# Gate and up products of an FFN: one product of 512 columns and one of 256 in place of three of 256

## Chip, cores and metric

The kernel runs on one core of one Trainium2 chip. The metric is the device time of one execution in microseconds. Every number in this part is of the kernel before the change.

## The reference

Two model blocks are computed one behind the other on 256 tokens of width 1024, each block with two layers. All is float32. Only the feed-forward networks (FFNs) are touched by the change:

```python
D_MODEL, SEQ, DEPTH, D_FF = 1024, 256, 2, 2816

def swiglu(x, w_gate, w_up, w_down):                 # first block
    return (jax.nn.silu(x @ w_gate) * (x @ w_up)) @ w_down

def _swiglu(h, w_in, w_out):                         # second block
    g, u = jnp.split(h @ w_in, 2, axis=-1)
    return (jax.nn.silu(g) * u) @ w_out

# first block, each layer
x = layer_norm(ALPHA * x + 0.5 * swiglu(x, ffn1...), ...)
...  # in-projection, pooling, convolution, attention, out-projection, layer_norm
x = layer_norm(ALPHA * x + 0.5 * swiglu(x, ffn2...), ...)
# second block, each layer
x = x + 0.5 * _rmsnorm(_swiglu(_rmsnorm(x, ng[0]), w_ffn_in[l, 0], w_ffn_out[l, 0]), ng[1])
...  # three mixers, branch gates, attention to a memory
x = x + 0.5 * _rmsnorm(_swiglu(_rmsnorm(x, ng[6]), w_ffn_in[l, 1], w_ffn_out[l, 1]), ng[7])
```

So there are eight FFNs: two in each of two layers of each of two blocks.

## The kernel before

**High and low halves.** TensorE takes float32r operands, which hold fewer bits than float32. To keep the precision, each operand is split in two: the high half is the value rounded to float32r, and the low half is the rest. A product is then the sum of three matmuls into the same PSUM bank: high by high, high by low, low by high. The helper `three` (L389, L390, L391) issues them for a weight of 128x128 and an activation of 128 (contraction) by 256 (tokens); its `left` is the weight's pair, its `right` the activation's pair. `three_rows` (L405 to L407) does the same with 512 moving columns. In it the activation is the stationary operand and the weight streams.

**Weight pieces.** Weights come in pieces of 128x1024 values (512 KB). A piece goes through four steps in the order of its number e. SyncE issues its DMA into one of 6 raw buffers (`sp_load`, L354). ScalarE copies it with rounding into `w_hi`, one of 3 slots (`act_split`, L702); for this it waits until piece e-3 has been used. VectorE subtracts it into `w_lo` (`low_part`, L913). TensorE waits for `split_low` and multiplies.

**The activations** of an FFN lie transposed in `in_hi` and `in_lo`, 8 tiles (KD) of 128 features by 256 tokens.

**An FFN** (`pe_ffn`, `act_ffn`, `dve_ffn`) runs over 22 tiles of 128 hidden features. Each tile has three pieces: gate, up and down. In steady state TensorE runs gate(j), up(j), down(j-1), gate(j+1), and so on. Gate and up take 8 values of k times `three`, 24 matmuls a piece; both results share a PSUM bank, `FFN_BANK[j % 2]`, as its two halves. Down takes 12 matmuls of 512 columns, from `hid_hi` and `hid_lo`, and accumulates in banks 0 to 3 over all tiles. Tile 0 is done by `begin`, which goes through gate and up together, two k at a time, as the activations arrive.

**Beside TensorE.** The order on ScalarE and VectorE is written out by `ffn_steps`, which calls `after(e, ...)` once for each piece e. In the first block ScalarE takes the silu of the gate out of PSUM (L752), and `hidden` on VectorE multiplies it by the up result in PSUM (L1014), rounds it to `hid_hi` (L1016) and subtracts for `hid_lo` (L1018). In the second block the RMS norm's factor is folded in behind the products (`fold`): VectorE first multiplies gate and up by `rstd` out of PSUM into `gate_up` (L1002, L1004), and silu and `hidden` work on that. `rstd` is made by a small product, `spread`, after tile 0.

**Seeded starts.** In three of the four FFNs of the first block VectorE writes the scaled residual into banks 0 to 3 (`dve_ln_seed`, L1099 and L1104). The second half of that (`second_seed`) is issued in `after(2)`, and the first down step waits for it.

## Time and profile before

| | us |
|---|---|
| median of three runs | 2785.0 (2780.41, 2785.0, 2787.51) |
| the profiled execution | 2780.14 |
| its span, first to last instruction | 2778.3 |
| mean granted TensorE clock | 0.993 of full speed |

The rows below come from the profiled execution alone. PE is TensorE's matmuls, PEld its weight loads, DVE is VectorE, ACT ScalarE, POOL GpSimd, and SPq the queue that issues DMAs. Matmuls are pipelined: the record of one lasts until its last result is written, so records overlap, and the sum of their lengths is more than the time. In a timeline the first number is the start, the second the length. Idle time and its releaser stand in brackets.

### The profile page before, as it was taken

To read this page: it belongs to the slowest core of one execution; us is meant where nothing else is said; L and a number is where in the kernel's file an instruction comes from. 1 tells how busy PE (TensorE), PEld (TensorE's weight loads), DVE (VectorE), ACT (ScalarE), POOL (GpSimd) and SP (SyncE) were. 2 spreads that over 40 slices of the span, in tenths; PEclk is the share of its full clock that TensorE was granted. 3 is DMA by queue.
4 is the path that set the end of the run, shared out by engine and by line. 5 is a ranking of instruction groups with operands and counts; after the bars stand their busy time and mean duration, and the time that the engine had idled before them with its cause. 6 is when DMAs were issued, how large, how long until landed. Compare 5 with 4: busy or idle time off the path is not lost.

```text
span 2778.3 us, 51978 instructions
## 1 busy us (share of the span) xinstructions
PE 2707.1 (97%) x21524; PEld 2499.6 (90%) x21524; DVE 1708.8 (62%) x2552; ACT 1306.4 (47%) x1855; POOL 217.4 (8%) x95
## 2 busy tenths in 40 slices
PE   8999999999999999999999999999999999999998
PEld 7999699899978989999899898999999889989998
DVE  5557755755757566666742756667665763375666
ACT  4445543434454444456633456445446642455543
POOL 0000000000000000005225000000002422300000
PEclk9999999999999999999999999999999999999999
DMA  8765366577545656664323554666664421464664
GB/s 238 210 194 160 98 189 186 172 221 195 165 122 164 184 158 183 186 193 122 102 75 107 167 182 122 196 181 178 186 203 133 128 85 55 160 189 133 177 184 128
DMA packets 622972, 445.41 MB, mean 160 GB/s; under 512 B 28048, under 2 KB 589488, under 8 KB 622320
## 3 DMA queue, kind: packets, MB, share of 16 engines
q1 hardware_dynamic: 622832, 443.43, 54.6%
q8 instruction: 102, 1.67, 0.2%
q14 instruction: 38, 0.31, 0.0%
HBM read 442.32 MB, written 1.05 MB: 160 GB/s over the span
## 4 chain that ended last, share of the span: by engine, by line
PE 88%; DVE 9%; ACT 2%; issue 1%; DMA 0%; SPq 0%; DVEq 0%; ACTq 0%
PE ps L389 19%; PE ps L391 18%; PE ps L390 18%; PE ps L405 7%; PE ps L406 7%; PE ps L407 7%; DVE w_lo L913 2%; PE ps L687 1%; PE ps L663 1%; PE ps L1661 1%; PE ps L1651 1%; ACT sq L1153 1%; DVE moments L1066 1%; PE ps L1623 1%; DVE sq L970 1%
## 5 line engine op out<-in xcount | busy, mean ns | idle before, releaser
L389 PE MATMUL ps<-in_hi,w_hi 128*128 128x256 f32 x4352 | 1248.7, 287 | 33.5 <-DVE in_lo L990 10.7
L913 DVE TENSOR_TENSOR w_lo<-raw,w_hi 128x1024 fp32r<-128x1024 f32 x705 | 862.1, 1225 | 647.2 <-ACT w_hi L702 646.2
L391 PE MATMUL ps<-in_hi,w_lo 128*128 128x256 f32 x4352 | 1234.5, 284 | 0.0
L390 PE MATMUL ps<-in_lo,w_hi 128*128 128x256 f32 x4352 | 1234.4, 284 | 0.0
L702 ACT ACTIVATE w_hi<-raw 128x1024 fp32r<-128x1024 f32 x800 | 845.0, 1057 | 794.7 <-PE ps L391 545.0
L389 PEld LDWEIGHTS ps<-in_hi,w_hi 128*128 128x128 f32 x4352 | 837.0, 192 | 56.2 <-issue 11.7
L390 PEld LDWEIGHTS ps<-in_lo,w_hi 128*128 128x128 f32 x4352 | 837.2, 192 | 7.2 <-issue 0.5
L391 PEld LDWEIGHTS ps<-in_hi,w_lo 128*128 128x128 f32 x4352 | 836.9, 192 | 0.0
L913 POOL TENSOR_TENSOR w_lo<-raw,w_hi 128x1024 fp32r<-128x1024 f32 x90 | 216.9, 2412 | 2176.3 <-ACT w_hi L702 2176.3
L405 PE MATMUL ps<-w_hi,hid_hi 128*128 128x512 f32 x704 | 276.5, 393 | 1.1 <-DVE ps L1104 1.1
L406 PE MATMUL ps<-w_lo,hid_hi 128*128 128x512 f32 x704 | 276.1, 392 | 0.0
L407 PE MATMUL ps<-w_hi,hid_lo 128*128 128x512 f32 x704 | 274.1, 389 | 0.0
L407 PEld LDWEIGHTS ps<-w_hi,hid_lo 128*128 128x128 f32 x704 | 132.3, 188 | 28.7
L405 PEld LDWEIGHTS ps<-w_hi,hid_hi 128*128 128x128 f32 x704 | 132.9, 189 | 25.4 <-DVE ps L1104 2.4
L406 PEld LDWEIGHTS ps<-w_lo,hid_hi 128*128 128x128 f32 x704 | 132.9, 189 | 21.2
L752 ACT ACTIVATE work<-work 128x256 f32<-128x256 f32 x88 | 37.0, 420 | 198.1 <-DVE work L1002 198.1
L752 ACT ACTIVATE work<-ps 128x256 f32<-128x256 f32 x88 | 33.7, 383 | 154.3 <-PE ps L391 154.3
L961 DVE TENSOR_TENSOR in_lo<-arena,in_hi 128x512 fp32r<-128x512 f32 x44 | 31.7, 744 | 93.0 <-ACT in_hi L708 92.8
L1018 DVE TENSOR_TENSOR hid_lo<-work,hid_hi 128x256 fp32r<-128x256 f32 x176 | 74.9, 426 | 6.0
L405 PE MATMUL ps<-w_hi,in_hi 128*128 128x512 f32 x192 | 75.6, 394 | 1.1 <-ACT std L830 1.1
L407 PE MATMUL ps<-w_hi,in_lo 128*128 128x512 f32 x192 | 74.8, 390 | 0.0
L406 PE MATMUL ps<-w_lo,in_hi 128*128 128x512 f32 x192 | 74.8, 389 | 0.0
(341 smaller groups left out, 2693.8 us busy)
## 6 DMA issues: line engine op xcount, KB each, us to landing
raw<-in_w_ffn_in SPq DMA_DIRECT2D x176, 512.0 KB, 3.9
raw<-in_w_mix SPq DMA_DIRECT2D x112, 512.0 KB, 3.8
raw<-in_ffn_w_gate SPq DMA_DIRECT2D x88, 512.0 KB, 4.0
raw<-in_ffn_w_up SPq DMA_DIRECT2D x88, 512.0 KB, 3.8
raw<-in_ffn_w_down SPq DMA_DIRECT2D x88, 512.0 KB, 3.6
raw<-in_w_ffn_out SPq DMA_DIRECT2D x88, 512.0 KB, 4.2
raw<-in_w_in SPq DMA_DIRECT2D x40, 512.0 KB, 3.8
raw<-in_w_out SPq DMA_DIRECT2D x32, 512.0 KB, 3.8
```

The lines of the kernel that those rows point to most:

```text
L389: nc.tensor.matmul(o, lh, rh, start=first, stop=False, **kw)
L390: nc.tensor.matmul(o, lh, rl, start=False, stop=False, **kw)
L391: return nc.tensor.matmul(o, ll, rh, start=False, stop=last, **kw)
L405: nc.tensor.matmul(o, left_hi[:, tok], right_hi, start=first, stop=False, **kw)
L406: nc.tensor.matmul(o, left_hi[:, tok], right_lo, start=False, stop=False, **kw)
L407: return nc.tensor.matmul(o, left_lo[:, tok], right_hi, start=False, stop=last, **kw)
L663: mm = nc.tensor.matmul(ps[:, 4 + i % 2, t * S:(t + 1) * S], q, k, start=(m == 0), stop=(m == len(pieces) - 1))
L702: nc.scalar.activation(w_hi[:, e % SPLIT, :], raw[:, e % RAW, :], ACT.Copy).then_inc(sem("split_high"), 1)
L752: nc.scalar.activation(silu[:, up % 2, :], src, ACT.Silu).then_inc(sem("silu_ready"), 1)
L913: eng.tensor_tensor(w_lo[:, e % SPLIT, :], raw[:, e % RAW, :], w_hi[:, e % SPLIT, :].bitcast(F32), ALU.subtract)\
L961: nc.vector.tensor_tensor(in_lo[:, lo:hi, :], src[:, 2 * c:2 * c + 2, :], in_hi[:, lo:hi, :].bitcast(F32), ALU.subtract).then_inc(sem("in_ ...
L1018: nc.vector.tensor_tensor(hid_lo[:, j, :], hid[:, j, :], hid_hi[:, j, :].bitcast(F32), ALU.subtract)\
```

## The change

From tile 1 on, gate and up get a bank each (`gate_up_bank`, four banks in rotation). For each k the high half of the weight multiplies the high and the low activations in one matmul of 512 columns: `in_hi` and `in_lo` become the two halves of one tensor, `in_both`, so that they are next to each other for each k. Its first 256 results are high by high, the other 256 high by low. The low half of the weight by the high activations is then accumulated onto the first 256. So a piece has 16 matmuls in place of 24, and its result lies in two halves that have to be added.

For the sum, ScalarE copies the second half out of PSUM into `part` (in `taken`, semaphore `part_taken`), and VectorE adds it to the first half into `gate_up` (in `whole_of`, semaphore `summed`). In the second block VectorE then multiplies the sum in place by `rstd` (`scaled`). Silu and `hidden` read `gate_up` instead of PSUM. The gate's half is taken and added in `after(3j-1)`, the up's in `after(3j)`. Tile 0 keeps its three products and takes bank 4 (`FIRST_BANK`); the bank of `spread` moves from 6 to 5. The list of semaphore names is changed to match and left out here.

```diff
@@ -169,7 +169,8 @@
         ps = ctx.enter_context(nc.psum_tensor("ps", [P, 8, 512], F32))
         raw = sb("raw", [P, RAW, PIECE])
         w_hi, w_lo = (sb(n, [P, SPLIT, PIECE], F32R) for n in ("w_hi", "w_lo"))
-        in_hi, in_lo = (sb(n, [P, KD, S], F32R) for n in ("in_hi", "in_lo"))
+        in_both = sb("in_both", [P, KD, 2, S], F32R)
+        in_hi, in_lo = (in_both[:, :, i, :] for i in range(2))
         hid_hi, hid_lo = (sb(n, [P, 2, S], F32R) for n in ("hid_hi", "hid_lo"))
         const = sb("const", [P, CONST_N])
         ones = sb("ones", [P, S])
...
@@ -187,6 +188,7 @@
         att_p = work[:, 4 * S:12 * S].rearrange("p (b c t) -> p b c t", b=4, c=2)
         att_pT = work[:, 12 * S:16 * S].rearrange("p (b c t) -> p b c t", b=2, c=2)
         diag = work[:, 8 * S:9 * S].rearrange("p (t c) -> p t c", t=HALF)
+        part = work[:, 9 * S:13 * S].rearrange("p (j a t) -> p j a t", j=2, a=2)
         first_gains = sb("first_gains", [P, LAYERS, KD])
         spare = sb("spare", [P, 2])
         moments = sb("moments", [P, HALF, 2, 6])
...
@@ -427,7 +429,7 @@
 
         WARM_BANK = 7
         TURN_BANK = 4
-        SPREAD_BANK = 6
+        SPREAD_BANK = 5
 
         def pe_warm(pe, n):
...
@@ -469,7 +471,19 @@
         given = (in_hi, in_lo)
 
 
-        FFN_BANK = (4, 5)
+        FIRST_BANK = 4
+
+        def gate_up_bank(j, i):
+
+            return ps[:, 4 + 2 * (j % 2) + i, :]
+
+        def summed(f, j, i):
+
+            return 2 * (f * (TILES - 1) + j - 1) + i + 1
+
+        def scaled(fold, j, i):
+
+            return 2 * (fold * TILES + j) + i + 1
 
         def pe_ffn(pe, n, e0, chunk, seeds=None, fold=None):
...
@@ -486,23 +500,24 @@
                             pe.wait_ge(sem("split_low"), e0 + i + 1)
                         w = piece(e0 + i)
                         for k in (2 * c, 2 * c + 1):
-                            mm = three(ps[:, FFN_BANK[i // 2], i % 2 * S:(i % 2 + 1) * S], at2(w, ALL, k, ALL),
-                                       at2(given, ALL, k, ALL), k == 0 and i % 2 == 0, k == KD - 1, skip_group_check=True)
+                            mm = three(ps[:, FIRST_BANK, i * S:(i + 1) * S], at2(w, ALL, k, ALL),
+                                       at2(given, ALL, k, ALL), k == 0 and i == 0, k == KD - 1, skip_group_check=True)
                         if c == KD // 2 - 1:
                             mm.then_inc(sem("piece_used"), 1)
 
             def gate_up(j, it=0):
                 for i in range(2):
-                    if 2 * j + i < TOGETHER:
-                        continue
-                    e = e0 + max(3 * j - 1, 0) + i
+                    e = e0 + 3 * j - 1 + i
 
                     pe.wait_ge(sem("split_low"), e + 1 + it * RAW)
-                    w = piece(e)
+                    hi, lo = piece(e)
+                    bank = gate_up_bank(j, i)
                     for k in range(KD):
 
-                        mm = three(ps[:, FFN_BANK[j % 2], i * S:(i + 1) * S], at2(w, ALL, k, ALL), at2(given, ALL, k, ALL),
-                                   k == 0, k == KD - 1)
+                        nc.tensor.matmul(bank.rearrange("p (a t) -> p a t", a=2), hi[:, k, :], in_both[:, k, :, :], start=(k == 0),
+                                         stop=False, skip_group_check=True)
+                        mm = nc.tensor.matmul(bank[:, 0:S], lo[:, k, :], in_hi[:, k, :], start=False, stop=(k == KD - 1),
+                                              skip_group_check=True)
                     mm.then_inc(sem("piece_used"), 1)
 
             def down(j, it=0, last=False):
...
@@ -738,17 +753,29 @@
         def act_ffn(act, n, e0, fold=None):
 
 
-            def after(e, up=None, whole=None, it=0):
+            def taken(e, i, j, it):
+
+                act.wait_ge(sem("piece_used"), e0 + e + 1 + it * RAW)
+                nc.scalar.activation(part[:, j % 2, i, :], gate_up_bank(j, i)[:, S:2 * S], ACT.Copy)\
+                    .then_inc(sem("part_taken"), 1)
+
+            def after(e, up=None, whole=None, it=0, gate=None):
+                if gate:
+                    taken(e, 0, gate, it)
+                if up:
+                    taken(e, 1, up, it)
                 if up == 0 and fold is not None:
                     act.wait_ge(sem("spread_ready"), fold + 1)
                     nc.scalar.activation(rstd[:, :], ps[:, SPREAD_BANK, 0:S], ACT.Copy).then_inc(sem("rstd_ready"), 1)
                 if up is not None:
+                    src = gate_up[:, up % 2, 0, :]
                     if fold is not None:
-                        act.wait_ge(sem("gate_scaled"), fold * TILES + up + 1 + it * 2)
-                        src = gate_up[:, up % 2, 0, :]
+                        act.wait_ge(sem("scaled"), scaled(fold, up, 0) + it * 4)
+                    elif up:
+                        act.wait_ge(sem("summed"), summed(ffn0 + n, up, 0) + it * 4)
                     else:
-                        act.wait_ge(sem("piece_used"), e0 + e + 1 + it * RAW)
-                        src = ps[:, FFN_BANK[up % 2], 0:S]
+                        act.wait_ge(sem("piece_used"), e0 + e + 1)
+                        src = ps[:, FIRST_BANK, 0:S]
                     nc.scalar.activation(silu[:, up % 2, :], src, ACT.Silu).then_inc(sem("silu_ready"), 1)
                 if e < FFN_PIECES - 1 and e0 + e + SPLIT < E_LAST:
                     act_split(act, e0 + e + SPLIT, it)
...
@@ -765,7 +792,7 @@
                     after(0)
                     after(1, 0, 0)
                     return
-                after(3 * j - 1, None, None, it)
+                after(3 * j - 1, None, None, it, gate=j)
                 after(3 * j, j, None, it)
                 after(3 * j + 1, None, j, it)
...
@@ -994,22 +1021,33 @@
         def dve_ffn(dve, n, e0, second_seed=lambda: None, fold=None):
 
 
-            def scaled(e, up, it):
-                j = up % 2
-                if up == 0:
-                    dve.wait_ge(sem("rstd_ready"), fold + 1)
-                dve.wait_ge(sem("piece_used"), e0 + e + 1 + it * RAW)
-                nc.vector.tensor_tensor(gate_up[:, j, 0, :], ps[:, FFN_BANK[j], 0:S], rstd[:, :], ALU.mult)\
-                    .then_inc(sem("gate_scaled"), 1)
-                nc.vector.tensor_tensor(gate_up[:, j, 1, :], ps[:, FFN_BANK[j], S:2 * S], rstd[:, :], ALU.mult)\
-                    .then_inc(sem("up_scaled"), 1)
+            def first_scaled(e):
+
+                dve.wait_ge(sem("rstd_ready"), fold + 1)
+                dve.wait_ge(sem("piece_used"), e0 + e + 1)
+                for i in range(2):
+                    nc.vector.tensor_tensor(gate_up[:, 0, i, :], ps[:, FIRST_BANK, i * S:(i + 1) * S], rstd[:, :], ALU.mult)\
+                        .then_inc(sem("scaled"), 1)
+
+            def whole_of(e, i, j, it):
+
+                o = gate_up[:, j % 2, i, :]
+                dve.wait_ge(sem("part_taken"), summed(ffn0 + n, j, i) + it * 4)
+                nc.vector.tensor_tensor(o, gate_up_bank(j, i)[:, 0:S], part[:, j % 2, i, :], ALU.add).then_inc(sem("summed"), 1)
+                if fold is not None:
+                    dve.wait_ge(sem("summed"), summed(ffn0 + n, j, i) + it * 4)
+                    nc.vector.tensor_tensor(o, o, rstd[:, :], ALU.mult).then_inc(sem("scaled"), 1)
 
             def hidden(whole, it):
                 j, count = whole % 2, (ffn0 + n) * TILES + whole + 1 + it * 2
+                up = gate_up[:, j, 1, :]
                 if fold is not None:
-                    dve.wait_ge(sem("up_scaled"), fold * TILES + whole + 1 + it * 2)
+                    dve.wait_ge(sem("scaled"), scaled(fold, whole, 1) + it * 4)
+                elif whole:
+                    dve.wait_ge(sem("summed"), summed(ffn0 + n, whole, 1) + it * 4)
+                else:
+                    up = ps[:, FIRST_BANK, S:2 * S]
                 dve.wait_ge(sem("silu_ready"), count)
-                up = ps[:, FFN_BANK[j], S:2 * S] if fold is None else gate_up[:, j, 1, :]
 
                 nc.vector.tensor_tensor(hid[:, j, :], silu[:, j, :], up, ALU.mult).then_inc(sem("hidden_whole"), 1)
                 dve.wait_ge(sem("hidden_whole"), count)
...
@@ -1018,9 +1056,13 @@
                 nc.vector.tensor_tensor(hid_lo[:, j, :], hid[:, j, :], hid_hi[:, j, :].bitcast(F32), ALU.subtract)\
                     .then_inc(sem("hidden_ready"), 1)
 
-            def after(e, up=None, whole=None, it=0):
-                if up is not None and fold is not None:
-                    scaled(e, up, it)
+            def after(e, up=None, whole=None, it=0, gate=None):
+                if up == 0 and fold is not None:
+                    first_scaled(e)
+                elif up:
+                    whole_of(e, 1, up, it)
+                elif gate:
+                    whole_of(e, 0, gate, it)
                 if up == 0 and fold is None:
 
                     hidden(whole, it)
```

## Rows read from the trace of the kernel before

**Rows 1.** The page, parts 1 and 2: busy time, and the granted clock in 40 slices.
```profile
PE 2707.1 (97%) x21524; PEld 2499.6 (90%) x21524; DVE 1708.8 (62%) x2552; ACT 1306.4 (47%) x1855; POOL 217.4 (8%) x95
...
PEclk9999999999999999999999999999999999999999
```

**Rows 2.** The page, part 4: the chain that ended last, by engine and line.
```profile
PE 88%; DVE 9%; ACT 2%; issue 1%; DMA 0%; SPq 0%; DVEq 0%; ACTq 0%
PE ps L389 19%; PE ps L391 18%; PE ps L390 18%; PE ps L405 7%; PE ps L406 7%; PE ps L407 7%; DVE w_lo L913 2%; PE ps L687 1%; PE ps L663 1%; PE ps L1661 1%; PE ps L1651 1%; ACT sq L1153 1%; DVE moments L1066 1%; PE ps L1623 1%; DVE sq L970 1%
```

**Rows 3.** The page, part 5: groups, with count, busy us, mean ns, idle before.
```profile
L389 PE MATMUL ps<-in_hi,w_hi 128*128 128x256 f32 x4352 | 1248.7, 287 | 33.5 <-DVE in_lo L990 10.7
...
L752 ACT ACTIVATE work<-work 128x256 f32<-128x256 f32 x88 | 37.0, 420 | 198.1 <-DVE work L1002 198.1
L752 ACT ACTIVATE work<-ps 128x256 f32<-128x256 f32 x88 | 33.7, 383 | 154.3 <-PE ps L391 154.3
```

**Rows 4.** Timeline of TensorE, one tile, first block: start us, us, engine, line, operation.
```profile
151.35 0.40 PE L405 MATMUL ps<-w_hi,hid_hi 128*128 128x512 f32 x1
151.59 0.40 PE L406 MATMUL ps<-w_lo,hid_hi 128*128 128x512 f32 x1
...
152.74 0.39 PE L405 MATMUL ps<-w_hi,hid_hi 128*128 128x512 f32 x1
...
154.10 0.28 PE L389 MATMUL ps<-in_hi,w_hi 128*128 128x256 f32 x1
154.21 0.28 PE L390 MATMUL ps<-in_lo,w_hi 128*128 128x256 f32 x1
...
159.85 0.40 PE L405 MATMUL ps<-w_hi,hid_hi 128*128 128x512 f32 x1
```

**Rows 5.** Busy time by stretch: one tile of each block, columns in the first row.
```profile
core 0: us, PE busy (x) PEld busy (x) DVE busy (x) ACT busy (x) POOL busy (x), PEclk, DMA share, GB/s
151.35:159.85 8.50, 8.50 (x62) 8.01 (x61) 4.73 (x6) 3.45 (x4) 0.00 (x0) 1.00 0.74 199
1803.00:1811.50 8.50, 8.50 (x62) 8.01 (x62) 5.49 (x8) 3.49 (x4) 0.00 (x0) 1.00 0.63 184
```

**Rows 6.** Timeline of ScalarE and VectorE in the tile of rows 4.
```profile
151.55 0.38 ACT L752 ACTIVATE work<-ps 128x256 f32<-128x256 f32 x1 [1.82 <-PE ps L391]
...
152.92 1.23 DVE L913 TENSOR_TENSOR w_lo<-raw,w_hi 128x1024 fp32r<-128x1024 f32 x1 [1.93 <-ACT w_hi L702]
...
156.53 0.41 DVE L1014 TENSOR_TENSOR work<-work,ps 128x256 f32<-128x256 f32 x1
...
157.31 0.43 DVE L1018 TENSOR_TENSOR hid_lo<-work,hid_hi 128x256 fp32r<-128x256 f32 x1
```

**Rows 7.** Timeline, last tile of an FFN of the second block, all engines.
```profile
2764.77 0.42 DVE L1002 TENSOR_TENSOR work<-ps,rstd 128x256 f32<-128x256 f32 x1 [0.50 <-PE ps L391]
...
2765.23 0.42 ACT L752 ACTIVATE work<-work 128x256 f32<-128x256 f32 x1 [2.22 <-DVE work L1002]
...
2765.75 0.42 DVE L1014 TENSOR_TENSOR work<-work 128x256 f32<-128x256 f32 x1 [0.22 <-ACT work L752]
...
2766.53 0.43 DVE L1018 TENSOR_TENSOR hid_lo<-work,hid_hi 128x256 fp32r<-128x256 f32 x1
...
2767.32 0.39 PE L405 MATMUL ps<-w_hi,hid_hi 128*128 128x512 f32 x1
```

**Rows 8.** Timeline at a seeded FFN start: TensorE, then VectorE.
```profile
345.65 0.50 PE L405 MATMUL ps<-w_hi,hid_hi 128*128 128x512 f32 x1 [0.37 <-DVE ps L1104]
...
342.87 1.40 DVE L1099 SCALAR_TENSOR_TENSOR zT<-ps,mean_var,arena 128x512 f32<-128x512 f32 x2
...
346.23 3.50 DVE L913 TENSOR_TENSOR w_lo<-raw,w_hi 128x1024 fp32r<-128x1024 f32 x3
```

**Rows 9.** The same, with the columns of rows 5, of one slow stretch.
```profile
280.00:287.00 7.00, 6.87 (x20) 3.93 (x19) 5.57 (x14) 4.56 (x13) 0.00 (x0) 0.55 0.43 146
```

More of the change, by code:

```diff
@@ L162, in build @@
                  "split_high", "split_low", "piece_used", "in_high", "in_ready", "turn_in", "turned", "rows_out", "silu_ready",
-                 "hidden_whole", "hidden_high", "hidden_ready", "tok_stat", "tok_std", "x_ready", "post_scaled", "diag_ready", "spread_ready", "rstd_ready", "gate_scaled", "up_scaled", "vector_step", "ln_here",
+                 "hidden_whole", "hidden_high", "hidden_ready", "tok_stat", "tok_std", "x_ready", "post_scaled", "diag_ready", "spread_ready", "rstd_ready", "scaled", "part_taken", "summed", "vector_step", "ln_here",
                  "gains_here", "ln_cols_here", "opened", "seeded", "ln_scale", "ln_turned", "ln_act", "ln_vec", "post_here0", "post_here1", "post_here2", "post_here3") + \
```

## Prediction

> **What bounds the kernel now.** I read the busy times and the granted clock first. TensorE is busy for 97% of the span, VectorE for 62%, ScalarE for 47%, and the clock row is at 9 tenths or more in all 40 slices [rows 1]. Then the chain that ended last: 88% of it is TensorE, 9% VectorE, 2% ScalarE, and three lines of one helper, L389 to L391, hold 19, 18 and 18% of the span [rows 2]. Those are the 128x256 products that the change rewrites. So wherever TensorE runs without a gap, what the change gives is what it takes out of TensorE's own stream; work added on VectorE and ScalarE counts only where TensorE then waits for it.
>
> The recorded mean of a matmul can't be used for its price: it is 287 ns at L389 [rows 3], while the products start every 120 ns, so the records overlap. I take differences of start times. Between the first gate product of a tile at 154.10 and the first down product at 159.85 lie 48 products of 256 columns: 5.75/48 = 0.1198 us each. The 12 products of 512 columns of the down step go from 151.35 to 154.10: 0.2292 each; the last six of them, from 152.74, take 1.36/6 = 0.2267, and the first six 1.39/6 = 0.2317 [rows 4]. The period of a tile is 8.50 us, in which TensorE is always busy, in the first block and in the second alike [rows 5].
>
> So one product of 512 columns with the same weights costs 0.2267 where two of 256 cost 2 x 0.1198 = 0.2396. The whole case for the change is this difference of 12.9 ns; twice the columns are still streamed.
>
> **What the change takes out.** Per weight piece and k, three products of 256 columns become one of 512 and one of 256. The silu appears 88 + 88 = 176 times, once a tile, so eight FFNs of 22 tiles [rows 3]. Tile 0 of each keeps the old form, which leaves 8 x 21 x 2 pieces x 8 k = 2688 such triples. Old price: 3 x 0.1198 = 0.3594. New price from the settled rows: 0.2267 + 0.1198 = 0.3465. Saving: 12.9 ns x 2688 = 34.7 us. No row of before shows 512 and 256 columns in turn, so this is the unknown cost. From below: the first 256-column product behind a run of 512 starts its successor after only 0.11 (154.10 to 154.21), which would make a pair 0.337 and the saving 61 us. From above: the first 512 behind a run of 256 takes 0.24 (151.35 to 151.59), a pair of 0.36 and no saving; the mean of the first six gives 0.3515, 7.9 ns and 21 us [rows 4]. In the new order each 512 follows a 256 and each 256 follows a 512, so the two edge effects (0.24 up, 0.11 down) meet in every pair: 0.35 together. That is why I take the settled 0.3465 and neither end.
>
> **What it adds on ScalarE.** One copy of 128x256 out of PSUM for each of the 336 pieces. The nearest row is the silu from PSUM with the same size, 0.38 us [rows 6]. Per tile that is 0.76 on an engine that is busy 3.45 to 3.49 of 8.50 [rows 5]. Behind it in the queue stands the split of the piece three further on, so that starts 0.38 later after a gate. Who waits: the subtraction (L913), and behind it TensorE. For the up piece, the subtraction starts at 152.92 and takes 1.23, done at 154.15; TensorE needs this piece only after the gate, 24 products behind 154.10, at 156.98 [rows 4, 6]. Slack 2.8 us, against a delay of 0.4: nothing reaches TensorE. In the second block the silu of a tile no longer waits for a multiplication behind the up piece, because the gate is finished earlier; that returns about what the up copy takes.
>
> **What it adds on VectorE.** One addition per piece, nearest row the product that reads PSUM, 0.41 [rows 6]. In the second block the multiplication by rstd stays as a second step (0.42) [rows 7]; it needs the addition's own result, so there is a wait of VectorE on itself as well. Busy per tile goes from 4.73 to about 5.6 in the first block and from 5.49 to 6.3 in the second, of 8.4 [rows 5]. The nearest deadline in the steady loop is hid_lo: it starts at 157.31 and ends at 157.74, and the down step starts at 159.85 [rows 4, 6]. Slack 2.1 us against at most 0.4 + 0.4 + 0.4. Hidden.
>
> **Where the cover is thin.** (a) Behind the last up piece of an FFN only one down step covers the chain. In the second block it ends in hid_lo at 2766.53 + 0.43 = 2766.96, and the last down step starts with the product at 2767.32: slack 0.36 [rows 7]. The old chain before the hidden product was two multiplications from 2764.77 and a silu from 2765.23, giving the product at 2765.75; the new one is copy 0.38, addition 0.42, multiplication 0.42 in sequence, so from 2764.75 to about 2766.0. That is 0.25 to 0.4 later: I charge 0.1 for each of four, 0.4 in all. In the first block silu and hid run without the multiplication and the cover is wider. (b) In three of the four FFNs of the first block VectorE also seeds the residual, and there TensorE waits for it: the seeding starts at 342.87, TensorE's down step idles until 345.65 for it, and w_lo follows from 346.23 [rows 8]. The change puts the addition for the gate of tile 1 ahead of the seeding, and it waits for ScalarE's copy of that gate; queued behind it are the seeding and the next w_lo. The gate is long done by 342.87, so the price is the addition, 0.38 to 0.42, three times: 1.2 us. The 16 pairs of tile 1 in each of these starts gain nothing either, because TensorE waits anyway: 48 x 12.9 ns = 0.6.
>
> **Other edits, at nothing.** Gate and up use four banks (4 to 7) in place of two; each is read out before the down step two tiles on, and the down step's existing waits order it. The spread moves to bank 5, whose old user was tile 1. in_hi and in_lo become halves of one tensor: the same 256-column runs, with a stride. No DMA is added or moved. A tile of 8.3 us in place of 8.5 asks 2.5% more of the DMA engines, which are at 0.63 to 0.74 [rows 5].
>
> **Sum.** 34.7 - 0.4 - 1.2 - 0.6 = 32.5 us less. The profiled execution took 2780.14 (span 2778.3) and would take 2747.6; the median of the three runs stands 4.9 higher, at 2785.0, and the forecast for it is 2785.0 - 32.5 = 2752.5, rounded to 2752.
>
> **Rivals.**
> 1. *The pair runs tighter*, at 0.337 to 0.343: the load of the 256-column product's weights is fully hidden behind a 512, and the 256 run was slowed by loads. For it: the 0.11 behind a run of 512 [rows 4]. Against: the 512 run pays as much over its columns although it leaves more time for a load. Saving 44 to 61 us, less 2.2: 2726 to 2743. The Trainium skill, "TensorE: Matmul & The Clock Gate", section "LDWEIGHTS (loading the stationary operand)", lets a load take its columns over 1.2, an estimate of 107 ns for 128 columns, which would speak for this rival; the load records here are no judge, at 192 ns each they overlap too.
> 2. *The pair pays the start-of-run price*, 0.3515: saving 21.2, less 2.2: 2766. For it: the slow first six [rows 4].
> 3. *No saving*: the 12.9 ns belong to a change of form and come back in each pair (0.24 + 0.12 = 0.36): 2785.0 + 0.4 + 1.2 = 2787. Against it: the 0.11 row, in the other direction. The Trainium skill, same page, section "Back-to-back issue gap", gives columns over 2.4 plus a fixed 2.5 ns; by that the edit would save only 2.5 x 2688 = 6.7 us and end at 2780, also no measurable change. The trace speaks against the figure: 0.2267 and 0.1198 lie 13 ns over 512/2.4 and 256/2.4, not 2.5.
> 4. *Slower: a wait comes into the loop.* Copy, addition and multiplication stretch the chain from the up piece to hid_lo. It decides from the slack of 2.1 us on [rows 4, 6]. All four new operations of a tile in sequence make 1.6, or 2.0 with two multiplications. If each took half as long again (2.9), the down step would start 0.8 late in each of 168 tiles: +134 - 32, so 2887. Against it: only half of them lie behind the up piece.
>
> **Chances.** Forecast (pair 0.344 to 0.349, 2743 to 2762) 0.66; rival 1 0.11; rival 2 0.13; rival 3 0.06; rival 4 0.04. A change of under 0.3% (8.4 us) can't be told from none by measurement. Faster: 0.66 + 0.11 + 0.13 = 0.90; same 0.06; slower 0.04. The range takes in rival 2 and most of rival 1. Beside this, the runs of before alone spread over 7 us, and a stretch in which the clock is at half level (280 to 287 us, 0.55 [rows 9]) can come or go with the phase of the gaps, at up to 3.5 us each: 2731 to 2771.
>
> **What would show it.** In the profile after: the start of each 512 of the gate and the next 512 some 0.3465 apart; a tile period of 8.50 - 16 x 0.0129 = 8.29; TensorE without waits in the loop; the w_lo and hid_lo still done ahead of their products; at the seeded starts 0.4 more idle. It is wrong if the pair is not 0.3465, and by 2.7 us for each nanosecond; or if TensorE waits for hid_lo or w_lo in the loop.

## The result, and the profile after

The changed kernel takes 2770.05 us (median of 8 runs, 2768.06 to 2781.79), against 2786.26 for the kernel before beside it (8 runs, 2780.41 to 2790.07). The ratio is 0.9945, 95% interval [0.9929, 0.9961]: 15.3 us faster, or 11 to 20. The forecast was 32.5 us less. The time itself is inside the forecast's range of 2731 to 2771, at its upper end; the gain is about half of what was worked out.

The page of the kernel after: busy time, the chain by engine, and four groups of part 5.

```profile
PE 2695.6 (97%) x18836; PEld 2357.5 (85%) x18836; DVE 1843.0 (67%) x2888; ACT 1401.6 (51%) x2191; POOL 217.4 (8%) x95
...
PE 88%; DVE 8%; ACT 2%; issue 1%; DMA 0%; SPq 0%; DVEq 0%; ACTq 0%
...
L517 PE MATMUL ps<-in_both,w_hi 128*128 128x512 f32 x2688 | 956.3, 398 | 1.7 <-DVE w_lo L940 1.6
L519 PE MATMUL ps<-in_both,w_lo 128*128 128x256 f32 x2688 | 754.2, 281 | 0.0
...
L759 ACT ACTIVATE work<-ps 128x256 f32<-128x256 f32 x336 | 129.5, 385 | 537.9 <-PE ps L519 537.9
...
L1036 DVE TENSOR_TENSOR work<-ps,work 128x256 f32<-128x256 f32 x336 | 142.0, 423 | 105.8 <-ACT work L759 103.3
```

Against [rows 1 to 3]: TensorE is still busy for 97% and still holds 88% of the chain. L517 and L519 are the new products, 2688 of each as counted. The copy (L759) and the addition (L1036) appear 336 times, at 385 and 423 ns each, where 0.38 and 0.41 to 0.42 us had been taken. VectorE went from 62 to 67%, ScalarE from 47 to 51%.

Busy time of one tile in each block, columns as in [rows 5]:

```profile
151.95:160.34 8.39, 8.39 (x45) 7.15 (x44) 5.59 (x9) 4.03 (x6) 0.00 (x0) 1.00 0.74 202
1799.00:1807.39 8.39, 8.39 (x46) 7.15 (x45) 6.29 (x11) 4.04 (x7) 0.00 (x0) 1.00 0.60 187
```

The tile's period is 8.39 us and TensorE is busy in all of it, as before. No wait came into the loop. But the period was to be 8.29. Over 168 tiles the 0.1 between them is 16 us, and that is the miss of the medians. The timeline of TensorE for one tile's gate and up, to be read beside [rows 4]:

```profile
151.95 0.39 PE L517 MATMUL ps<-in_both,w_hi 128*128 128x512 f32 x1
152.18 0.28 PE L519 MATMUL ps<-in_both,w_lo 128*128 128x256 f32 x1
152.29 0.40 PE L517 MATMUL ps<-in_both,w_hi 128*128 128x512 f32 x1
152.53 0.28 PE L519 MATMUL ps<-in_both,w_lo 128*128 128x256 f32 x1
152.64 0.40 PE L517 MATMUL ps<-in_both,w_hi 128*128 128x512 f32 x1
...
157.59 0.40 PE L407 MATMUL ps<-w_hi,hid_hi 128*128 128x512 f32 x1
```

16 pairs take 157.59 - 151.95 = 5.64, so 0.3525 each, where 0.3465 was forecast. From the starts: the first 512 takes 0.23 and the second 0.24, the 256s 0.11. The hundredths only hint at the series. Its medians, taken in ns over the 160 tiles between the first and the last down step of the eight FFNs, are 227, 113 and then, again and again, 233, 117, 241, 120, 236, 113: three pairs in 1060, 353.3 each.

### The profile page after: what moved, and what is told of

Read it like the earlier page. It is cut to its first block, busy times and chain, and to the rows that moved or that the text cites. A ratio compares the mean times of both kernels' runs of the same rounds, so it can differ in the third digit from the quotient of the medians.

```text
span 2768.2 us, 47826 instructions
## 1 busy us (share of the span) xinstructions
PE 2695.6 (97%) x18836; PEld 2357.5 (85%) x18836; DVE 1843.0 (67%) x2888; ACT 1401.6 (51%) x2191; POOL 217.4 (8%) x95
## 4 chain that ended last, share of the span: by engine, by line
PE 88%; DVE 8%; ACT 2%; issue 1%; DMA 0%; SPq 0%; DVEq 0%; ACTq 0%
PE ps L517 22%; PE ps L519 11%; PE ps L391 8%; PE ps L393 7%; PE ps L392 7%; PE ps L407 7%; PE ps L408 7%; PE ps L409 7%; DVE w_lo L940 2%; PE ps L702 1%; PE ps L678 1%; PE ps L1703 1%; PE ps L1693 1%; ACT sq L1195 1%; PE ps L1665 1%
## 5 line engine op out<-in xcount | busy, mean ns | idle before, releaser
L517 PE MATMUL ps<-in_both,w_hi 128*128 128x512 f32 x2688 | 956.3, 398 | 1.7 <-DVE w_lo L940 1.6
L519 PE MATMUL ps<-in_both,w_lo 128*128 128x256 f32 x2688 | 754.2, 281 | 0.0
L517 PEld LDWEIGHTS ps<-in_both,w_hi 128*128 128x128 f32 x2688 | 505.1, 188 | 126.2 <-DVE w_lo L940 3.4
L391 PE MATMUL ps<-in_both,w_hi 128*128 128x256 f32 x1664 | 488.2, 293 | 31.7 <-DVE in_both L1017 10.7
L519 PEld LDWEIGHTS ps<-in_both,w_lo 128*128 128x128 f32 x2688 | 507.5, 189 | 6.2
L393 PE MATMUL ps<-in_both,w_lo 128*128 128x256 f32 x1664 | 474.0, 285 | 0.0
L392 PE MATMUL ps<-in_both,w_hi 128*128 128x256 f32 x1664 | 473.9, 285 | 0.0
L759 ACT ACTIVATE work<-ps 128x256 f32<-128x256 f32 x336 | 129.5, 385 | 537.9 <-PE ps L519 537.9
L391 PEld LDWEIGHTS ps<-in_both,w_hi 128*128 128x128 f32 x1664 | 322.0, 194 | 46.9 <-issue 11.5
L392 PEld LDWEIGHTS ps<-in_both,w_hi 128*128 128x128 f32 x1664 | 322.1, 194 | 1.0 <-issue 0.5
L393 PEld LDWEIGHTS ps<-in_both,w_lo 128*128 128x128 f32 x1664 | 321.8, 193 | 0.0
L1036 DVE TENSOR_TENSOR work<-ps,work 128x256 f32<-128x256 f32 x336 | 142.0, 423 | 105.8 <-ACT work L759 103.3
L988 DVE TENSOR_TENSOR in_both<-arena,in_both 128x512 fp32r<-128x512 f32 x44 | 31.8, 745 | 93.8 <-ACT in_both L723 93.6
```

The costliest lines, as they stand in the source:

```text
L391: nc.tensor.matmul(o, lh, rh, start=first, stop=False, **kw)
L392: nc.tensor.matmul(o, lh, rl, start=False, stop=False, **kw)
L393: return nc.tensor.matmul(o, ll, rh, start=False, stop=last, **kw)
L517: nc.tensor.matmul(bank.rearrange("p (a t) -> p a t", a=2), hi[:, k, :], in_both[:, k, :, :], start=(k == 0), stop=False, skip_group_check ...
L519: mm = nc.tensor.matmul(bank[:, 0:S], lo[:, k, :], in_hi[:, k, :], start=False, stop=(k == KD - 1), skip_group_check=True)
L759: nc.scalar.activation(part[:, j % 2, i, :], gate_up_bank(j, i)[:, S:2 * S], ACT.Copy)\
```

## The experiments

Each experiment stands beside runs of the kernel before of its own set: median 2786.24 us for three256, all512, by_two and by_eight, 2780.25 for skewed, by_four, mirrored and seed_first, and one run of 2780.45 for the three narrow ones. So a time is compared with its own set first, and what a tile takes is read from the traces.

Theories at the start. A: each change of size between neighbouring products has a price. B: after a switch of size there is a transient of several products, as in the first six of the down step [rows 4]. C: the price is not in the order but in the operands: w_hi and w_lo in turn, the whole bank written, the strided halves.

**Undo the 512 and keep all else** (`three256`).

```diff
-nc.tensor.matmul(bank (512 columns), hi[:, k, :], in_both[:, k, :, :], start=(k == 0), ...)
+nc.tensor.matmul(bank[:, 0:S], hi[:, k, :], in_hi[:, k, :], start=(k == 0), ...)
+nc.tensor.matmul(bank[:, S:2 * S], hi[:, k, :], in_lo[:, k, :], start=False, ...)
```

> The change with its layout, banks, copy and addition kept, but the product of 512 columns undone: high by high and high by low are two products of 256 into the two halves of the bank. A tile's gate and up then have 48 products again. Theory A (the price lies in products of 512 and 256 columns in turn): three products take 0.359 to 0.360 us as before, 5.75 a tile, and the time is that of before plus what copy and addition cost at the seeded starts and behind the last up piece, 2 to 4 us more. Theory C (the price lies in the new bank layout or the strided halves): the products stay slower than 0.120 each, and the time is 10 us or more above before.

Measured: 2787.14 us against 2786.24, ratio 1.0004 [0.9991, 1.0017]; the 2 to 4 us expected can't be told from nothing in the times. TensorE in one tile, first product, second, and the first of the down step:

```profile
154.41 0.28 PE L517 MATMUL ps<-in_both,w_hi 128*128 128x256 f32 x1
154.52 0.28 PE L519 MATMUL ps<-in_both,w_hi 128*128 128x256 f32 x1
...
160.16 0.40 PE L407 MATMUL ps<-w_hi,hid_hi 128*128 128x512 f32 x1
```

48 products in 5.75, 0.1198 each, as before. Banks, layout, copy and addition cost TensorE nothing within the loop. From the start of the first down step to the start of the tenth product of the last one, the eight FFNs take 1402.9 us together against 1400.9 before: what the side work costs there is 2.0 us. In the kernels compared this way, no stretch at half clock falls into these loops. C has lost its layout and its banks.

**One size, weights still alternating** (`all512`).

```diff
-mm = nc.tensor.matmul(bank[:, 0:S], lo[:, k, :], in_hi[:, k, :], ...)
+mm = nc.tensor.matmul(bank (512 columns), lo[:, k, :], in_both[:, k, :, :], ...)
```

> The low half of the weight also multiplies both halves of the activations, 512 columns, so all products of gate and up have one size; this adds the product low by low, which the change leaves out, to the second half of the bank. Weights still alternate between w_hi and w_lo. Theories A and B (size in turn): every product takes the settled 0.2267, a pair 0.453, the tile's gate and up 7.25, the time about 2770 + 168 x 1.61 = 3040. Theory C (w_hi and w_lo in turn, or the whole bank being written): a pair keeps the surplus of 6 ns or more, 0.460, the tile 7.35, the time about 3057.

Measured: 3032.5 us. Each product takes 226.7 ns from its start to the next one's, the tile's gate and up 7.253, and the down step behind it 2.720 instead of 2.747: its slow first six are gone, because no 256 stands before them. w_hi and w_lo in turn cost nothing. C is out. That the time is 7.5 us under the 3040 expected is mostly the down step, 168 x 0.027 = 4.5, and the longer tiles also cover waits at the seeded starts: the three first down steps there take 3.07, 2.99 and 2.76 us, against 4.16, 3.85 and 3.81 in the kernel after, 3.0 us less.

The trace of all512 shows one thing more. At the last down step of an FFN in the second block, TensorE has to wait, and there is no product of 256 anywhere near:

```profile
3019.14 0.39 PE L409 MATMUL ps<-w_hi,hid_lo 128*128 128x512 f32 x1
3019.55 0.47 PE L407 MATMUL ps<-w_hi,hid_hi 128*128 128x512 f32 x1
3019.86 0.39 PE L408 MATMUL ps<-w_lo,hid_hi 128*128 128x512 f32 x1
```

The products at 3019.14 and 3019.55 take 0.41 and 0.31, which is the wait. Those behind them then take 229, 233, 236, 224, 231, 236, 228, 233 and 231 ns, and only then 227. So slow products of 512 follow a wait as they follow products of 256: a change of size is one disturbance of the stream among others.

**The order by blocks** (`by_two`, `by_eight`): two of 512, two of 256, and so on; or all eight of 512 and then all eight of 256. The products and their operands are unchanged.

```diff
-for k in range(KD):          # high k (512 columns), low k (256 columns)
+for (low, k) in [(low, k + c) for k in range(0, KD, 2) for low in range(2) for c in range(2)]:   # by_two
+for (low, k) in [(low, k) for low in range(2) for k in range(KD)]:                               # by_eight
```

> Two products of 512, then two of 256, and so on, instead of one and one; same products, same operands. After shows 5.640 for a tile's gate and up (16 pairs of 0.3525; settled they would take 5.544). Theory A (a price for each change of size): half the changes, so half the surplus of 96 ns: 5.59 a tile, 8 us less than after. Theory B (a transient of some five products behind each change, as the first six of a down step): no settling within two, 5.64 or more, the same time as after.

> All eight products of 512 of a piece, then all eight of 256. Theory A: one pair of changes per piece, 5.544 + 2 x 0.006 = 5.556 a tile, 14 us less than after, about 2756. Theory B: each switch to 512 pays the 28 ns of a down step's first six and each switch back wins 7, so 5.544 + 2 x 0.021 = 5.586 a tile, 9 us less than after, 2761. Theory C (it isn't the order): 5.64, the same as after.

Measured: by_two 2752.0 (one run), by_eight 2755.68, ratio 0.9888 [0.9872, 0.9905]. TensorE in one tile of by_eight; rows with x8 hold eight products:

```profile
150.97 1.98 PE L522 MATMUL ps<-in_both,w_hi 128*128 128x512 f32 x8
152.78 1.11 PE L519 MATMUL ps<-in_both,w_lo 128*128 128x256 f32 x8
153.73 2.00 PE L522 MATMUL ps<-in_both,w_hi 128*128 128x512 f32 x8
155.57 1.11 PE L519 MATMUL ps<-in_both,w_lo 128*128 128x256 f32 x8
156.53 0.40 PE L407 MATMUL ps<-w_hi,hid_hi 128*128 128x512 f32 x1
```

150.97 to 156.53 is 5.56 (median 5.559). The same products in another order are 81 ns a tile faster than in the kernel after. But by_two has four times as many switches as by_eight and takes 5.563, almost the same. A's 5.556 fits by_eight, but its 5.59 for by_two doesn't come, so there is no one price for a switch. B fails on both: 5.64 was expected for by_two and 5.586 for by_eight. In by_eight the first eight 512 stand behind a down step and take 227 each; the second eight, behind 256s, take 233, 236, 228, 233, 231, 227, 227, 227; each eight of 256 takes 113, 119, then 120. What costs most is one and one.

**Operands again, and four by four** (`skewed`, `by_four`).

```diff
-for (low, k) in [(0, 0), (1, 0), (0, 1), (1, 1), ...]
+for (low, k) in [(low, (k + 4 * low) % KD) for k in range(KD) for low in range(2)]               # skewed
+for (low, k) in [(low, k + c) for k in range(0, KD, 4) for low in range(2) for c in range(4)]    # by_four
```

> 512 and 256 columns one by one as in after, but the product of the weight's low half takes another k (k + 4, modulo 8), so that no activation is streamed twice in a row. Theory D (the surplus of the one-by-one order lies in the operands: the 256 columns just streamed are read again, or the same k of both weight halves): the surplus falls, a tile's gate and up go from 5.640 toward the 5.563 of by_two. Theory E (the order of sizes alone sets it): 5.640, with the same series of 233, 117, 241, 120, 236, 113 ns.

> Four products of 512, then four of 256. The trace of by_eight shows what a switch does: the 512 behind 256 take 233, 236, 228, 233, 231 and then 227 ns, the 256 behind 512 take 113, 119 and then 120. Theory E1 (each run begins its series anew, and the costs add up): 4 x 227 + 472, then three times 930 + 472, 5.586 a tile, more than by_two with half as many switches. Theory A (each change has one price): between the 5.563 of by_two and the 5.559 of by_eight.

Measured: skewed 2769.7 and by_four 2767.6 (one run each). TensorE in one tile of skewed:

```profile
151.84 0.39 PE L522 MATMUL ps<-in_both,w_hi 128*128 128x512 f32 x1
152.06 0.28 PE L519 MATMUL ps<-in_both,w_lo 128*128 128x256 f32 x1
...
157.48 0.40 PE L407 MATMUL ps<-w_hi,hid_hi 128*128 128x512 f32 x1
```

157.48 - 151.84 = 5.64 again, with the series of the kernel after. Theory E holds: the sizes' order sets it, not what is read. by_four has a median of 5.587 a tile where adding up the series had given 5.586, and A's 5.559 to 5.563 fails. That the sum fits so closely is in part chance: inside its later runs the series is a different one (118, 119, 117, 117 for the 256s, then 235, 233, 236, 224 for the 512s), with nearly the same total.

**Narrower weights.** Why should the order of sizes matter? Theory L: a product of 256 columns is too short to cover the load of the next weights. Which load stands beside which product is shown by the kernel after (PEld is a load; it begins with the product beside it):

```profile
152.18 0.28 PE L519 MATMUL ps<-in_both,w_lo 128*128 128x256 f32 x1
152.18 0.19 PEld L517 LDWEIGHTS ps<-in_both,w_hi 128*128 128x128 f32 x1
```

Beside the short product the high half's weights for the next 512 are loaded, and beside the 512 the low half's.

```diff
+def wide(k): return 64 if 0 < k < KD - 1 else P
-hi[:, k, :]   and   lo[:, k, :]
+hi[:, k, 0:wide(k)]   and   lo[:, k, 0:wide(k)]      # narrow and narrow256; narrow_high: hi alone
 # the results of such a product go to bank[0:wide(k)]; narrow and narrow_high start from after, narrow256 from three256
```

> three256 with weights of 64 columns instead of 128 in the products of k = 1 to 6, so the other 64 hidden features of a tile get only the terms of k = 0 and 7: a quarter of the features' work is left out of the sums, the columns streamed stay the same. Settled products of 256 columns at full clock take 106.7 ns of streaming (256 / 2.4) and 0.120 is measured. Theory L (the 13 ns over the columns are the load of the next weights, which a smaller load shortens): 0.110 or less at k = 1 to 6. Theory F (a fixed price of each product, whatever it loads): 0.120 throughout, the tile's gate and up 5.753.

> after, with the same 64 weight columns at k = 1 to 6 in both halves of the weight, 512 and 256 columns still one by one. Theory L: the surplus of the one-by-one order is loads that don't fit, so pairs fall from 0.353 to under 0.3465, toward 0.33. Theory F: the series 233, 117, 241, 120, 236, 113 stays, 5.640 a tile.

> after, with 64 columns only for the high half of the weight at k = 1 to 6, the load that happens beside the short product of 256; the low half's load, beside the 512, keeps 128. Theory L: as in narrow, since only the load beside the short product can be late; the pair is under 0.3465. Theory F: 5.640 a tile. If narrow falls and this one doesn't, the price is in the load of the low half beside the 512.

Nine products of narrow256, all with weights of 64 columns, from the first row to the last (the second row shows the next start):

```profile
151.53 0.28 PE L520 MATMUL ps<-in_both,w_hi 128*64 128x256 f32 x1
151.64 0.28 PE L522 MATMUL ps<-in_both,w_hi 128*64 128x256 f32 x1
...
152.55 0.28 PE L520 MATMUL ps<-in_both,w_hi 128*64 128x256 f32 x1
```

(152.55 - 151.53)/9 = 0.1133: with half the load, 256 columns stream in 113 ns and not in 120. F falls. L has the mechanism and not the number: 0.110 or less was expected, because the columns were taken at 106.7 ns. And 2 x 113.3 = 226.6, the 226.7 of a product of 512: there is no fixed price per product to be seen; a float32r column costs 0.443 ns in both lengths, and the rest of the 120 was the load. The load records shrink with the weights, from 188 to 194 ns on average for 128 columns to this:

```profile
L522 PEld LDWEIGHTS ps<-in_both,w_hi 128*64 128x64 f32 x2016 | 270.1, 134 | 0.0
```

Now narrow_high, high products with 128*64, low ones with 128*128:

```profile
151.42 0.39 PE L520 MATMUL ps<-in_both,w_hi 128*64 128x512 f32 x1
151.65 0.28 PE L522 MATMUL ps<-in_both,w_lo 128*128 128x256 f32 x1
151.76 0.39 PE L520 MATMUL ps<-in_both,w_hi 128*64 128x512 f32 x1
...
152.10 0.39 PE L520 MATMUL ps<-in_both,w_hi 128*64 128x512 f32 x1
```

(152.10 - 151.42)/2 = 0.34, that is 227 + 113 ns, in narrow the same. Only the load of the high half, which runs beside the short product, was cut here, and the whole surplus of the one-by-one order went. Narrow weights also halve the results that a product writes. That isn't what counts: here the products of 256 write all 128 rows of results and take 113 ns, and in all512 full products of 512 take 227. Around k = 7 and the k = 0 behind it, where weights are full, slower pairs remain: 350 to 360 ns in narrow_high, 344 to 350 in narrow. The opposite cut, the low half's load alone, was not run. Run times, one each: narrow256 2751.2, narrow 2745.0, narrow_high 2754.7.

**The order that follows from it** (`mirrored`), and VectorE's seeding ahead of the addition (`seed_first`).

```diff
-for (low, k) in [(low, k) for low in range(2) for k in range(KD)]
+for (low, k) in [(low, k) for low in ((0, 1), (1, 0))[i] for k in range(KD)]      # mirrored; i = 0 gate, 1 up
 # seed_first, beside it, in dve_ffn's after():
+if e == 2 and up is None and whole is None: second_seed()     # now ahead of whole_of(e, 0, gate, it)
```

> Gate: eight of 512, eight of 256; up: eight of 256, eight of 512, so that a tile with its down step has one switch up in size instead of two. By the series above: gate and up 16 x 0.2267 + 16 x 0.120 - 0.008 + 0.028 = 5.567, and the down step behind it settled, 12 x 0.2267 = 2.720 instead of 2.747. A tile 8.287 against 8.306 in by_eight: 3 us less than by_eight's 2755.7, about 2752.5. If instead the transient belongs to the start of a down step (its operands are swapped, weights stream) and not to the size before it, the down step stays at 2.747 and the time at 2757.

> mirrored, with VectorE's second seeding put ahead of the first addition. Theory of the seeded starts (the addition ahead of the seeding delays TensorE by its own length at three starts): at those starts the down step's wait falls by 0.38 us each, 1.1 us in all against mirrored, too little for the clock time and plain in the trace. Rival (the wait is set by the seeding of before, not by the addition): no change in the wait.

Measured: mirrored 2758.71 (6 runs, 2751.34 to 2761.91), ratio 0.9914 [0.9898, 0.993]; seed_first 2753.64 (5 runs), ratio 0.9901 [0.9885, 0.9917]. Both stand beside 2780.25 for before. TensorE in one tile of mirrored:

```profile
150.58 1.98 PE L522 MATMUL ps<-in_both,w_hi 128*128 128x512 f32 x8
152.40 2.08 PE L519 MATMUL ps<-in_both,w_lo 128*128 128x256 f32 x16
154.31 2.00 PE L522 MATMUL ps<-in_both,w_hi 128*128 128x512 f32 x8
156.15 0.39 PE L407 MATMUL ps<-w_hi,hid_hi 128*128 128x512 f32 x1
...
158.87 1.98 PE L522 MATMUL ps<-in_both,w_hi 128*128 128x512 f32 x8
```

Gate and up take 156.15 - 150.58 = 5.57, and the down step 158.87 - 156.15 = 2.72. Both are as expected: the transient comes from what stands before the down step, and not from the down step itself. The run times can't rank mirrored, seed_first, by_two and by_eight. Four of the six runs of mirrored have a mean clock of 0.989 or less, and they are the four above 2758; the two of 0.990 and 0.991 are at 2753.2 and 2751.3. The 2752.5 expected for mirrored lies between those two, and its median is 6 us over it. The FFN loops can be ranked, all eight together and measured as for three256, in the profiled executions (gate and up, down step: medians):

| kernel | FFN loops, us | gate and up of a tile, us | down step, us |
|---|---|---|---|
| before | 1400.9 | 5.753 | 2.747 |
| three256 | 1402.9 | 5.753 | 2.747 |
| after, skewed | 1385.4, 1385.3 | 5.640 | 2.747 |
| by_four | 1379.8 | 5.587 | 2.767 |
| by_eight | 1372.4 | 5.559 | 2.748 |
| by_two | 1370.4 | 5.563 | 2.730 |
| mirrored | 1369.4 | 5.567 | 2.720 |
| seed_first | 1368.9 | 5.567 | 2.720 |

So a change of order alone, with every product kept, takes the loops from 15.5 to 31.5 us under those of before. At the same seeded start, the down step's wait for the seeding, first in the kernel after (in mirrored it is 0.8 as well) and then in seed_first:

```profile
PE ps L407 <- DVE ps L1146: 0.8, 1, 0.8
```

```profile
PE ps L407 <- DVE ps L1149: 0.5, 1, 0.5
```

It fell from 0.8 to 0.5, not by the 0.38 of the addition, and at the first such start 0.3 came back as a wait for w_lo: the second and third of these loops are 0.2 us shorter than in mirrored, the first is not. So 0.5 us came of the 1.1 expected: the seeding theory has the right sign and half its size.

## Why the prediction was right and wrong

**The bound: right.** TensorE's stream sets the time, and the loop has no wait, in the kernel before as in the one after.

**The price of the pair: the step that failed.** The difference of 12.9 ns between 0.2267 and twice 0.1198 was read as a price per product, and the pair was put at 0.2267 + 0.1198 = 0.3465. It is no price per product. 512 columns pay streaming alone, 226.7; 256 columns stream in 113.3 and wait 7 for the load of the next 128 weight columns (narrow256 against three256). In the new order one load of two still stands beside a short product. The 512 behind it starts its successor late, 233 to 241, and the pair is 352.5. So the saving is 168 x (5.753 - 5.640) = 19.0 us and not 34.7. The edge rows of both kinds had been seen [rows 4], and it was argued that they add up to 0.35, but 0.3465 was then taken, the value of runs that never alternate. Nor would the edges have given the answer. The 0.24 is a reading in hundredths; over all tiles of before the first 512 behind a 256 takes 233 ns and the first 256 behind a 512 takes 114, together 347. No row of before has the two lengths one by one, and the series of 233, 241 and 236 came only with that order. So the price was open, as the prediction said, and its chance of 0.66 for 0.344 to 0.349 was too high.

**Rival 2 came nearest, by luck.** Its 0.3515 is the slow 512 of 0.2317 with a 256 of 0.1198. In the new series the 512s average 236.7 and the 256s 116.7, so both parts are off, in opposite directions. That the time fell into the stated range owes something to this too: the range took in rival 2, and the allowance for the clock was put on top.

**Rival 1 had the mechanism and not the number.** It said that the runs of 256 are slowed by loads. The argument held against it, that a 512 pays as much over its columns, took the columns at 2.4 GHz for granted; narrow256 shows 256 columns at 0.443 ns each, no less. Its pair of 0.340 is what narrow weights give. The Trainium skill, "TensorE: Matmul & The Clock Gate", section "LDWEIGHTS (loading the stationary operand)", lets the load take its columns over 1.2, an estimate of 107 ns for 128 and 53 for 64. The runs agree that the price goes with the weight's columns: the load record is 54 ns shorter with 64 of them (188 and 134). They don't agree that 107 ns is all that counts, since that would fit beside the 113 of a product of 256, and 128 columns hold such a product back to 120; with 64 it isn't held back at all.

**Rival 3 and rival 4: rightly small.** The pair is under 0.36, no fixed part shows in 113.3 and 226.7 ns, and no wait came into the loop.

**The side work: nearly right in sum, not in its parts.** Forecast at 0.4 + 1.2 us; three256 shows 2.0 in the FFN loops. The three seeded ones take 0.3 each of it (1.2 charged, 1.0 measured), the four of the second block 0.26 each (0.4 charged, 1.0 measured). The thin cover behind the last up piece, in an FFN of the second block of the kernel after:

```profile
2754.80 0.42 DVE L1036 TENSOR_TENSOR work<-ps,work 128x256 f32<-128x256 f32 x1 [0.63 <-ACT work L759]
...
2755.72 0.42 DVE L1052 TENSOR_TENSOR work<-work 128x256 f32<-128x256 f32 x1
...
2756.51 0.43 DVE L1056 TENSOR_TENSOR hid_lo<-work,hid_hi 128x256 fp32r<-128x256 f32 x1
2756.70 0.39 PE L409 MATMUL ps<-w_hi,hid_lo 128*128 128x512 f32 x1
...
2757.08 0.47 PE L407 MATMUL ps<-w_hi,hid_hi 128*128 128x512 f32 x1
...
2757.39 0.39 PE L408 MATMUL ps<-w_lo,hid_hi 128*128 128x512 f32 x1
```

Against [rows 7]: copy, addition (2754.80), multiplication, then the hidden product at 2755.72. hid_lo ends at 2756.94. TensorE's product at 2756.70 takes 0.38 and the one at 2757.08 0.31, where 0.23 is normal: a wait of 0.23, where 0.1 had been charged for each FFN. Around the start of the first down step these FFNs wait for about 0.2 as well (245 and 305 ns for two products that take 117 and 241 in the first FFN, where nothing waits), which the forecast had overlooked. At the seeded starts the wait for the seeding went from 0.4 to 0.7 and 0.8, as charged.

**From the pair to the span.** Between the first and last down step lie 20 tiles, 160 in all: 160 x 0.113 = 18.1, less 2.0, makes 16.1; the table has 15.5. The rest, 0.6, lies in the eight first down steps: 25.97 us together in the kernel after, 25.38 in three256. From the start of tile 1's gate to the end of the first down step, seven of the eight FFNs take the same in both kernels, within 0.04 us: what tile 1 saves there is spent again in waits and in the slow products behind them. The forecast had let tile 1 gain nothing at the three seeded starts alone. Of the 19.0 us, the side work's 2.0 and those seven tiles' 0.8 leave 16.2, the difference of the medians. One FFN of the second block, the first product of the first down step and the tenth of the last, before and after:

```profile
1726.69 0.40 PE L405 MATMUL ps<-w_hi,hid_hi 128*128 128x512 f32 x1
...
1901.47 0.39 PE L405 MATMUL ps<-w_hi,hid_hi 128*128 128x512 f32 x1
```

```profile
1722.45 0.47 PE L407 MATMUL ps<-w_hi,hid_hi 128*128 128x512 f32 x1
...
1895.35 0.39 PE L407 MATMUL ps<-w_hi,hid_hi 128*128 128x512 f32 x1
```

174.78 became 172.90. Outside the loops the profiled execution after is 5.4 us longer, so its gain is 10.1 and not 15.5. The clock is the reason as far as it can be seen. By estimate, a mean granted clock of 0.993 over 2778.3 us is 19.4 us of clock not granted, and 0.991 over 2768.2 is 24.9, that is 5.5 more. In three stretches of the kernel after, columns as in [rows 5], the granted clock (PEclk) is near half.

```profile
275.00:289.00 14.00, 11.95 (x31) 6.81 (x32) 9.53 (x25) 8.51 (x27) 0.00 (x0) 0.51 0.31 108
1353.50:1357.50 4.00, 4.00 (x11) 1.13 (x10) 2.54 (x6) 2.96 (x6) 0.00 (x0) 0.57 0.81 226
1541.00:1545.20 4.20, 4.20 (x25) 4.20 (x24) 4.17 (x7) 0.03 (x1) 0.00 (x0) 0.59 0.02 3
```

The first is the stretch of [rows 9], there 7 us long and here 14. In before the clock was full around the other two (1.00 at 1358 to 1362 and at 1545 to 1549). The forecast had allowed up to 3.5 us for each such stretch that comes or goes, and that held. The gain of the medians, 16.2, depends on the clock of the runs beside it too: before's run at a mean clock of 0.993 in the set of three256 took 2780.06 us, and those at 0.990 and 0.991 took 2785.65 to 2787.18. The 15.5 us of the loops don't depend on it.

## What to carry to other kernels

When a short product stands between weight loads, the price of a mix can't be read from runs of one length, and not from single transitions either: here these give 346.7 and 347 ns a pair, and the mix costs 352.5. Run the mix itself, in a small kernel or in one tile, before it is priced. If products of two lengths share a loop, group them by length, and mirror the order so that neighbouring groups have the same length; in the FFN loops that alone was worth as much again as the change (16.0 us beside 15.5). Before a constant excess is called a price per instruction, halve the load and see whether it stays.

## What the runs showed of the hardware

Float32r columns stream at 0.443 ns each, in products of 256 (113.3 ns, narrow256) and of 512 (226.7, all512) alike: 13 ns over 512 / 2.4, and no fixed part. With weights of 128 columns a run of 256-column products is paced by loads at 120 ns. After a run of 256 a 512 pays 6 ns more and settles only after five products (233, 236, 228, 233, 231, 227), and one and one never settles (352.5 a pair, against 348 in two and two). A wait leaves such slow products behind it as well, without any product of 256 (all512: 306, 229, 233, 236, 224, 231, 236, 228, 233, 231, 227). How loads and products together make these series is open: no run here shows it, and the load records (188 to 194 ns with 128 columns) overlap too much to say, since loads start 113 to 120 ns apart where products of 256 run.
